# Waits, one table's load and filler products moved in a two-block transformer kernel

## The reference

```python
def first_block(x, c, ctx, ...):            # DEPTH = 1
    hx = modulate(rms_norm(x, g_mix), mod_x[0], mod_x[1]);  hc = ... the same for ctx
    mx = gated_merge(gates, retention(hx, hc), window(hx, hc), neighbourhood(hx, hc), ...)
    x = x + mod_x[2] * mx
    x = x + mod_x[5] * expert_choice_ffn(modulate(rms_norm(x, g_ffn), ...))
    return rms_norm(x, g_final)

def retention_readout(y, g, gn_gain):       # y: 4 heads x 128 wide
    mu = mean(y); var = mean(square(y - mu))
    return (y - mu) * rsqrt(var + EPS) * gn_gain * silu(g)

def expert_choice_ffn(h, w_router, w_gate, w_up, w_down):   # 16 experts, 64 tokens each
    aff = softmax(h @ w_router); gate, idx = top_k(aff.T, 64)
    hid = silu(h[idx] @ w_gate) * (h[idx] @ w_up)
    return zeros.at[idx].add((hid @ w_down) * gate)

def second_block(x, c, ctx, ...):           # DEPTH_2 = 2 layers
    for l in range(2):
        y_mla, y_pool = mla_branch(z, zc, ...), pool_branch(z, ...)
        y_gla = gla_branch(z, zc, af_w2, ...)   # gated linear attention, both directions
        out = (g1*(y_mla@w1) + g2*(y_pool@w2) + g3*(y_gla@w3)) @ w_out
        x = x + gate * rmsnorm(out, post_g);  ctx likewise in layer 0
# in gla_inputs, per direction: rank 16 -> 256 columns
log_a = log_sigmoid(z['gla_af'] @ af_w2 + af_b) / 16      # af_w2: (16, 256)
```

## Time and profile before

| | |
|---|---|
| Three timed runs | 3014.37, 3006.28, 3011.75 us; median 3011.75 |
| The profiled execution | 3010.27 us; span of its instructions 3008.5 us |
| Mean granted TensorE clock | 0.974 of full |
| TensorE busy | 2855.0 us, 95% of the span |
| VectorE, ScalarE, GpSimd busy | 993.3, 898.6, 645.0 us |
| Chain that ended last | TensorE 80%, transfers 8%, VectorE 4%, ScalarE 4% |

### The profile page before, as it was taken

How to read it: one execution, slowest core, us unless ns; L and a number is a source line. 1 busy time by engine, 2 the same in 40 slices (tenths; PEclk the granted TensorE clock), 3 DMA queues, 4 the chain that set the end, 5 groups by cost and what they waited for, 6 DMA issues and landing times.

```text
span 3008.5 us, 37694 instructions
## 1 busy us (share of the span) xinstructions
PE 2855.0 (95%) x15540; PEld 2133.5 (71%) x15540; DVE 993.3 (33%) x1431; ACT 898.6 (30%) x1364; POOL 645.0 (21%) x323
## 2 busy tenths in 40 slices
PE   6999999999989999999999999999998999999997
PEld 4856777788744433337899667999997888577886
DVE  3433421511252111113266543211134075643113
ACT  4222334522331111104333244211124333343223
POOL 1202012044410000001221002522222231006443
PEclk9999999999989999999999999999997999999999
DMA  6143113022369999993222002111133131003222
GB/s 251 70 193 151 44 51 118 16 97 98 140 248 417 422 422 422 422 421 129 79 81 81 30 1 92 57 70 57 62 107 126 56 107 65 29 8 123 89 97 98
DMA packets 64785, 424.73 MB, mean 141 GB/s; under 512 B 6848, under 2 KB 6848, under 8 KB 18176
## 3 DMA queue, kind: packets, MB, share of 16 engines
q1 hardware_dynamic: 52416, 375.41, 31.8%
q0 software_dynamic: 3808, 27.81, 2.4%
q10 hardware_dynamic: 8416, 19.40, 1.7%
HBM read 405.56 MB, written 17.04 MB: 140 GB/s over the span
## 4 chain that ended last, share of the span: by engine, by line
PE 80%; DMA 8%; DVE 4%; ACT 4%; issue 2%; POOL 1%; ACTq 0%; SPq 0%; DVEq 0%; POOLq 0%
PE psum L675 77%; DMA ring<-in_weights 5%; PE psum L678 3%; DMA late_slots<-in_weights 2%; ACT hidden_high L1682 1%; DMA residual<-in_acts 1%; DVE small L2220 1%; POOL weight_parts L2893 1%; ACT hidden L1676 0%; ACT arena L1691 0%; ACT arena L1713 0%; DMA arena<-in_t_count 0%; ACT weight_parts L1637 0%; ACT hidden L1675 0%; POOL arena L2987 0%
## 5 line engine op out<-in xcount | busy, mean ns | idle before, releaser
L675 PE MATMUL psum<-hidden_high,weight_parts 128*128 128x384 f32 (+2 forms) x3296 | 873.1, 365 | 28.5 <-DVE hidden_low L2171 12.8
L2893 POOL TENSOR_TENSOR weight_parts<-ring,weight_parts 128x1024 fp32r<-128x1024 f32 x218 | 537.8, 2468 | 1321.3 <-ACT weight_parts L1637 1301.1
L675 PEld LDWEIGHTS psum<-hidden_high,weight_parts 128*128 128x128 f32 x3296 | 607.5, 191 | 108.0 <-issue 21.9
L675 PE MATMUL psum<-hidden_low,weight_parts 128*128 128x384 f32 (+2 forms) x2160 | 653.7, 363 | 6.2 <-issue 4.6
L1637 ACT ACTIVATE weight_parts<-ring 128x1024 fp32r<-128x1024 f32 x218 | 230.5, 1059 | 1088.9 <-PE psum L675 1062.0
L675 PE MATMUL psum<-arena 128*64 128x128 f32 (+8 forms) x3120 | 496.8, 364 | 19.2 <-DMA arena<-in_weights 6.5
L675 PEld LDWEIGHTS psum<-hidden_low,weight_parts 128*128 128x128 f32 x2160 | 402.5, 190 | 46.9 <-issue 6.4
L675 PEld LDWEIGHTS psum<-arena 128*64 128x64 f32 (+3 forms) x3120 | 278.1, 159 | 179.6 <-issue 141.8
L1691 ACT ACTIVATE arena<-psum 128x512 f32<-128x512 f32 (+4 forms) x224 | 159.9, 720 | 394.6 <-PE psum L675 378.2
L2300 DVE TENSOR_TENSOR arena<-arena,psum 128x512 f32<-128x512 f32 (+1 forms) x72 | 55.9, 777 | 516.7 <-PE psum L675 515.9
L675 PE MATMUL psum<-ring,arena 128*64 128x512 f32 (+1 forms) x792 | 193.4, 600 | 14.9 <-DMA ring<-in_weights 13.2
(11 more groups left out here) (288 smaller groups left out, 2545.1 us busy)
## 6 DMA issues: line engine op xcount, KB each, us to landing
ring<-in_weights SPq DMA_DIRECT2D x260, 1024.0 KB, 6.7
late_slots<-in_weights SPq DMA_DIRECT2D x48, 1024.0 KB, 15.0
arena<-in_weights SPq DMA_DIRECT2D x48, 1024.0 KB, 17.2
spilled_projections<-arena ACTq DMA_DIRECT2D x14, 384.0 KB, 2.3
arena<-spilled_projections ACTq DMA_DIRECT2D x3, 1536.0 KB, 12.4
residual<-in_acts POOLq DMA_DIRECT2D x1, 3072.0 KB, 19.9
arena<-in_bias POOLq DMA_DIRECT2D x1, 3072.0 KB, 10.3
arena<-in_t_count POOLq DMA_DIRECT2D x2, 1536.0 KB, 11.0
```

Of the source, the lines that this page charges most:

```text
L675: return nc.tensor.matmul(o, lhsT, rhs, start=start, stop=stop)
L2893: G_.tensor_tensor(parts[:, i % 2, 1, :], tile_at(t), parts[:, i % 2, 0, :], ALU.subtract).then_inc(*E.sig("tile_split"))
```

## The change

1. Retention's 16 one-column sums go to bank 7, four per head, each head's after a wait of its own, with two slices (12 products) of the tile `k_w` behind each head's. VectorE and ScalarE wait for the new signals `head_sums` and `head_variances`.
2. The load of `t_win` moves on GpSimd ahead of the splits of `k_w` and the first `q_w`, and waits for retention's last products (`rS`, `rY`) and no longer for the stage's end.
3. Window attention: TensorE waits for each head's rotation before that head's scores, and for v_w's evacuation before the first outputs. ScalarE evacuates v_w ahead of the split that stood before it, and runs one Exp before that.
4. Neighbourhood attention: waits for q_n and k_n per head ahead of its scores, for the values before the first outputs. ScalarE evacuates k_n's last tile ahead of the split.
5. `w_out`: of the pair's second tile only slices 0 to 2 (not 0 to 5) stand ahead of the first tile's last two slices.
6. `keep_warm` is added: 5 after block 1's w_out, 2 after each of two hidden turns, 2 ahead of the slots, 3 ahead of the gathering, 5 after the last pair; in layer 1's chunks 7 ahead of chunks 3, 4 and 5 in place of 8 ahead of 3 and 5.
7. The decay's second product runs over all 128 rows of gSM; the weight tile is zero elsewhere, and the second direction lies at columns 256 to 511.

```diff
@@ w_out
+                ahead = (KT - 2, 3)
                 for f in range(2):
...
-                    for k in range(KT - 2):
+                    for k in range(ahead[f]):
@@ retention
-            pe.wait_ge(*E.next("head_squares", 4))
-            token_sums("ret", [rSq[:, h, :] for h in range(4)], range(4))
-
-            project_tile(("k_w", 0), ("k_w", 0), ALL)
+            hi, lo = weight_parts("k_w", 0)
+            ps, stat = group("k_w", 0), psum[:, 7 * 512:7 * 512 + 32]
+            for h in range(4):
+                pe.wait_ge(*E.next("head_squares"))
+                ins = columns_summed(stat, h, rSq[:, h, :], range(4))
+                if h == 3:
+                    ins.then_inc(sem("head_sums"), 1)
+                for k in (2 * h, 2 * h + 1):
+                    ins = tile_products(split(hi, a=KT), split(lo, a=KT), ps, k, ALL, (Hhi, Hlo))
@@ window
-            pe.wait_ge(*E.next("rotated", 5))
             pe.wait_ge(*E.next("window_keys_padded"))
             pe.wait_ge(*E.next("second_keys_padded"))
-            pe.wait_ge(*E.taken("v_w"))
+            def window_heads(t):
+                pe.wait_ge(*E.upto("rotated", keys_rotated + t + 1))
@@ neighbourhood
-            for t in range(4):
+            def neighbour_heads(t):
                 pe.wait_ge(*E.taken("q_n", t))
                 pe.wait_ge(*E.taken("k_n", t))
@@ feed-forward
             w_out(0, lambda f: ("w_out", f), IMG)
+            keep_warm(5)
...
                 hidden_turn(tt)
+                keep_warm(2)
...
+            keep_warm(2)
             pe.wait_ge(*E.next("slots_ready"))
...
+            keep_warm(3)
...
             pair("last", PAIRS - 1, PAIRS - 1, None)
+            keep_warm(5)
@@ decays
-                            ins = mm(ps[:, ci * 512:ci * 512 + n], w2[32 * d:32 * d + 16, t * P:(t + 1) * P],
-                                     gSM[32 * d:32 * d + 16, c0:c0 + n], True, True)
+                            ins = mm(ps[:, ci * 512:ci * 512 + n],
+                                     w2[:, (2 * d + t) * P:(2 * d + t + 1) * P], gSM[:, c0:c0 + n], True, True)
@@ chunks
-                    if l == 1 and c % 2:
-                        keep_warm(8)
+                    if l == 1 and c > 2:
+                        keep_warm(7)
@@ ScalarE, window
-            high()
+            act_(tick[:, 9:10], C("eps"), ACT.Exp)
             act.wait_ge(*E.next("window_values"))
             act_(wV.rearrange("p a n -> p (a n)"), cols("v_w")[:, 0:TOK], ACT.Copy).then_inc(*E.read("v_w"))
+            high()
@@ GpSimd
-            low(18)
+            low(14)
+            pool.wait_ge(*E.written("rS", 3, 2))
+            pool.wait_ge(*E.written("rY", 3))
+            pool.dma_start(area(WIN + 3584, 1024), dram["t_win"]).then_inc(sem("win_tables_loaded"), 16)
+            low(4)
...
-            pool.dma_start(area(WIN + 3584, 1024), dram["t_win"]).then_inc(sem("win_tables_loaded"), 16)
@@ host
-            out[i, 32:48, 0:256] = x["gla_ab_w2_2"][lead]
+            out[i, 32:48, 256:512] = x["gla_ab_w2_2"][lead]
```

61 lines of the change are left out of this document (38 added, 23 removed).

## The result

The changed kernel takes 2980.64 us in the median of four runs (2975.71 to 2984.35), the kernel before 3011.59 (3006.28 to 3014.37). The ratio is 0.9898, with a 95% interval of 0.9877 to 0.9919: 31 us less, clear of no change. The profiled execution is the fastest of the four, 2975.71 us with a span of 2973.9.

What follows compares the result with a forecast made beforehand. TensorE, busy 95% of the span, was taken to bound the kernel, leaving waits and half-clock stretches to win. Terms summed to 31.2 us, from a median of 3011.75 to 2980.55, taken as 2980; range from 2970 to just above 2997.

Steps and rivals of the forecast that it cites:

- window: Window attention: shorter TensorE waits for v_w's evacuation and the first softmax, plus kept clock; gain 3.4 us, bounds 2 and 4.5.
- neighbourhood: Neighbourhood attention: the 3.23 us wait for k_n's last evacuation goes, first turn waits 0.4 less; gain 3.6 us.
- retention: Retention's one-column sums: clock stays up (5.1 us), 0.86 of waiting goes, 0.4 lost; gain 5.5 us, bounds 1 and 6.
- the output pair: w_out: waits ahead of the third tile nearly vanish, less a new wait for merged parts; gain 5.1 us, bounds 3.5 and 6.
- the decays: Both layers' decays over all rows: clock gives 5.5 us, lost overlap costs 0.8; gain 4.7, bounds −2.5 and 6.
- the selection: Feed-forward's selection: nine fillings stand in waits, two can end after what they wait for; net −0.5 us, bounds −6 and +2.
- rival (f): Window: the PSUM slot's wait stays despite the change; already in the sum, so only 1.0 us stands there; no separate chance.
- rival (b): Decays: the number of rows has no part in the clock; −0.8 instead of 4.7 us, total 2986; chance 0.11.
- Rival (c): Selection: fillings stand in the path at half clock, 5.6 us more, total 2986; chance 0.12.
- (a): Retention, decays, chunks, statistics: clock falls at the same places all the same; 15 us of gain remain, 2997; chance 0.12.
- (d): First stage: transfers swallow the early gains through waits for weights; 3 to 4 us, total 2983; chance 0.06.
- (e): Expert loop: the shifted start lets the clock fall, slower than before; 3065 if in 60 units; chance 0.02.

## Why the prediction was right, point by point

**The number.** 2980 was forecast, 2980.6 measured. That is closer than the method is good for, and luck. Terms that were too small (window and neighbourhood, by 1.0 together, the tables by 0.3, retention by 0.1) and too large (the output pair by 0.6, the decays by 0.9, filling after w_out by 1.0, the selection by 0.6, the chunks by 0.2) leave a sum 1.9 too large; the places that the change doesn't touch happened to give 1.7.

**Waits.** Each wait that was named went or shrank, but for one at the neighbourhood. Tables: 8 us of slack were forecast, VectorE waits 5.98 for GpSimd's end of stage. The window's rival (f), that the slot's wait stays, was right as a mechanism: TensorE's new waits bring nothing there, and the order on ScalarE brings more than it was given, 2.39 for the two waits (forecast 2.2) and 1.66 behind them. The step that failed there is its size: "fewer idle microseconds keep the clock" was put at 1.2 and measured 1.66. The neighbourhood's 3.9 hang on TensorE's waits: without them 0.3 is left. There a step of the working was wrong though the sum came out near: the first turn was to come with 0.4 less of waiting. It waits 0.83 us more, 1.42 for 0.59. What pays for it is a term that wasn't in the sum, the clock: the 12 score products stood at half clock before and take 1.92 us instead of 3.31.

**The output pair.** The split's 3.7 us against 3.6 of cover left 0.23 and 0.25, near the 0.1 worked out. The step that was mis-sized is the new wait for the merged parts. It was put at 0.5 in each use with 512 columns; the shift falls by 0.72 there (by 0.52 at the wait itself, of which the row shows 0.34, and 0.20 one product pair later) and rises by 2.03 at the third tile. In layer 0 it doesn't arise, and 1.83 are won where 1.55 were forecast.

**Decays.** The reading that a product over few rows keeps the clock up less was the least sure step, with a rule against it. It holds at the two places: rival (b) is out, by the run over 16 rows in one group together with the one over 16 rows in two. That the gain reaches the end of the kernel is shown less well: in the kernel before the same edit brought 0.3 us (at most 3.6) in the time. The rule in the Trainium skill ("TensorE: Matmul & The Clock Gate", Part 1, "What's actually happening") that the gate goes by how busy TensorE was is not contradicted in its words, but busy time alone doesn't tell it: 3.31 of 3.40 us busy with 16 rows fell, 3.38 with 64 kept. What the same page of the Trainium skill says of row groups (Part 3, "The mechanism"), that products in different ones overlap, agrees with the traces: 12 records took 2.95 us side by side, 16 took 5.42 to 5.43 one behind another. Mis-sized was layer 1: 2.1 − 0.4 forecast, 0.8 measured, because of 3.1 us won there 1.3 and 1.0 go into two waits, the second for GpSimd's split (0.97 and 0.72 us at TensorE). That the wait on the scans would take part was said, its size wasn't.

**Retention and chunks.** Both are the order's and the fillings' doing, by the runs without them. Retention's 5.6 holds against the one profile of before; another execution with the old code there had 3.4 us less at half clock, and against such a one the order is worth 4.1. "No wait stands behind" chunk 5's fillings was right: 0.5 where 0.47 was put.

**Fillings in the selection.** Rival (c) had a chance of 0.12 and was partly what happened: fillings on the path at half clock. The forecast's −0.5 is −1.1 on average, within its bounds. The step that failed is that two of them can end after what they wait for: it counted the fillings' own time only. The 0.8 to 1.5 us by which the last weights come later were not in it at all. After w_out the half clock went from 6.8 us to 3.4 as hoped, but it did so in the three profiles without the five fillings too. The step that failed there is the 1.0 us given to the fillings for it: they brought nothing.

**Rivals (a), (d), (e).** The clock didn't fall at the filled places, transfers swallowed nothing in the first stage, and the expert loop stayed at 1.00 throughout in every profile.

**What stays open.** Some stretches at half clock (around 1330 to 1370, 1630 to 1660, 2260 to 2310, 2510 to 2560 and 2720 us) are longer or shorter by 3.4 us, at 2720 by up to 6.9, from one execution of the same kernel to the next. They make up the range of 8.6 us between the changed kernel's own runs, as far as its two profiles tell. What sets them wasn't tried. Also open are why the decays' gain doesn't show in the time of the kernel before, and whether fillings ahead of the gathering hold the clock. That the packet of instructions is what delays the landing is read from its standing there in every profile; no run moved it by itself.

## What to carry to other kernels

A filler product is free only if three things are free: its own time at the clock that it will really get, what waits behind it on its engine, and what waits for its engine elsewhere. Put it in a long wait ahead of heavy work, as ahead of chunk 4, and not ahead of a short product that another engine waits for. Check with a run without it that it was the filler that held the clock. And where the clock falls behind work that is busy all the time, look at the shape of that work: products over 16 rows or of one column may be worth widening or mixing with others. Take the gain from the time of the whole kernel in many executions, and not only from the place: time at half clock can come back elsewhere.

## What was not expected of the hardware

The number of rows that a product uses has a part in the granted clock: 16 records of 384 columns over 16 rows, 3.31 of 3.40 us busy, were followed by 10.20 us at 0.50; the same 16 over 64 rows, 3.38 of 3.40 us busy, by none. Padding with zeros serves: over 128 rows, of which 112 have zero weights in every product, the clock stayed too. 64 rows take the same time as 128, 5.42 and 5.43 us.

A packet of instructions, 16 KB in about 1 us on one of 16 DMA engines, stood in fourteen of fourteen profiles in the one gap between two landings of queued 1 MB units that was 0.8 to 1.6 us longer than the 2.5 of the others. It costs only where an engine is waiting for just that unit.
